# Joining the recurrence's triangular inverse to 128 rows, and applying it in one product per unit

## The reference, cut to what matters

```python
def step(state, inp):
    r_t, w_t, k_t, v_t, kk_t, b_t = inp
    sa = jnp.einsum('bhij,bhj->bhi', state, kk_t)
    state = (state * w_t[:, :, None, :]
             - sa[..., None] * b_t[:, :, None, :]
             + v_t[..., None] * k_t[:, :, None, :])
    y = jnp.einsum('bhij,bhj->bhi', state, r_t)
    return state, y
```

## Time and profile before

| | |
|---|---|
| median of 3 runs | 1575.68 us (1571.98 to 1575.98) |
| profiled execution: its time, its span | 1576.64 us, 1574.4 us |
| PE busy | 1473.1 us, 94% of the span |
| DVE, ACT, POOL busy | 739.1, 604.9, 464.0 us |
| mean granted clock of PE | 0.943 of full |
| recurrence, stages 15 to 22, batch 1 | about 148 to 177 us from the span's start |
| the same, batch 2 | about 298 to 376 us |

### The profile page before, as it was taken

One profiled execution on the slowest core, in us unless ns is written; L12 is line 12 of the kernel. 1 busy time (PEld: TensorE's weight loads), 2 busy tenths in 40 slices (PEclk: granted clock), 3 DMA queues, 4 the chain that ended last, 5 costly groups with the idle time before them and its releaser, 6 DMA issues.

```text
span 1574.4 us, 19313 instructions
## 1 busy us (share of the span) xinstructions
PE 1473.1 (94%) x7736; PEld 1154.6 (73%) x7736; DVE 739.1 (47%) x1156; ACT 604.9 (38%) x948; POOL 464.0 (29%) x162
## 2 busy tenths in 40 slices
PE   6999997899879999999998999999999988699995
PEld 5878876688668888888876887666687867577762
DVE  3356277733353532515132596334352335566663
ACT  4443245322353332323134124533333444255552
POOL 2352122000225664646423444320134520200002
PEclk9999998657899999999998999999999999799998
DMA  6232112000135445354432333200123521889964
GB/s 209 87 121 68 56 66 95 2 1 1 46 129 160 135 146 159 124 158 142 139 107 80 98 112 99 80 27 27 49 85 107 188 58 67 346 314 422 419 261 188
DMA packets 97803, 203.90 MB, mean 130 GB/s; under 512 B 6672, under 2 KB 56208, under 8 KB 91056
## 3 DMA queue, kind: packets, MB, share of 16 engines
q1 hardware_dynamic: 90656, 176.94, 32.6%
q10 hardware_dynamic: 4752, 17.30, 2.7%
q0 software_dynamic: 2304, 8.39, 1.4%
HBM read 168.54 MB, written 34.08 MB: 129 GB/s over the span
## 4 chain that ended last, share of the span: by engine, by line
PE 83%; DVE 6%; ACT 5%; issue 3%; DMA 2%; POOL 1%; SPq 0%; POOLq 0%; DVEq 0%; ACTq 0%
PE bank L517 21%; PE bank L499 12%; PE bank L501 12%; PE bank L500 12%; PE bank L2770 4%; PE bank L780 3%; PE bank L799 3%; PE bank L790 2%; PE bank L1193 2%; PE bank L782 1%; ACT whi L428 1%; PE bank L706 1%; PE bank L2716 1%; PE bank L1149 1%; PE bank L1252 1%
## 5 line engine op out<-in xcount | busy, mean ns | idle before, releaser
L436 POOL TENSOR_TENSOR wlo<-raw,whi 128x2048 fp32r<-128x2048 f32 (+2 forms) x83 | 378.7, 4562 | 698.1 <-ACT whi L428 672.0
L428 ACT ACTIVATE whi<-raw 128x2048 fp32r<-128x2048 f32 (+1 forms) x84 | 159.1, 1894 | 279.6 <-PE bank L501 272.1
L517 PE MATMUL bank<-alo,whi 128*128 128x512 f32 x368 | 149.5, 406 | 4.9 <-DVE alo L728 4.9
L1986 DVE TENSOR_TENSOR ffn_relu<-ffn_relu 128x512 f32<-128x512 f32 x32 | 97.7, 3052 | 107.0 <-ACT ffn_relu L1966 107.0
L517 PE MATMUL bank<-ahi,whi 128*128 128x512 f32 x368 | 146.5, 398 | 0.0
L499 PE MATMUL bank<-alo,whi 128*128 128x512 f32 (+1 forms) x360 | 141.1, 392 | 0.0
L501 PE MATMUL bank<-ahi,wlo 128*128 128x512 f32 (+1 forms) x360 | 140.3, 390 | 0.0
L500 PE MATMUL bank<-ahi,whi 128*128 128x512 f32 (+1 forms) x360 | 140.1, 389 | 0.0
L517 PE MATMUL bank<-ahi,wlo 128*128 128x512 f32 x368 | 91.7, 391 | 0.0
L517 PEld LDWEIGHTS bank<-alo,whi 128*128 128x128 f32 x368 | 71.3, 194 | 23.5 <-DVE alo L728 6.1
L517 PEld LDWEIGHTS bank<-ahi,whi 128*128 128x128 f32 x368 | 71.4, 194 | 15.5 <-issue 0.7
(11 more groups left out here) (483 smaller groups left out, 3005.2 us busy)
## 6 DMA issues: line engine op xcount, KB each, us to landing
raw<-in_w_in_dram SPq DMA_DIRECT2D x18, 1024.0 KB, 5.1
expert_gate_up<-in_expert_w_gate_dram SPq DMA_DIRECT2D x17, 1024.0 KB, 11.8
expert_gate_up<-in_expert_w_up_dram SPq DMA_DIRECT2D x17, 1024.0 KB, 14.2
expert_down<-in_expert_w_down_dram SPq DMA_DIRECT2D x17, 1024.0 KB, 9.2
raw<-in_w_ffn_up_dram SPq DMA_DIRECT2D x16, 1024.0 KB, 6.2
raw<-in_w_ffn_down_dram SPq DMA_DIRECT2D x16, 1024.0 KB, 5.6
raw<-in_w_in_first_dram SPq DMA_DIRECT2D x12, 1024.0 KB, 5.5
expert_rows_dram<-zero_rows SPq DMA_DIRECT2D x23, 512.0 KB, 6.9
```

The lines of the kernel that those rows point to most:

```text
L428: nc.scalar.activation(whi[:, n % SPLIT, 0:k * c], raw[:, n % RAW, 0:k * c], ACT.Copy).then_inc(hi_made, 1)
L436: nc.gpsimd.tensor_tensor(wlo[:, n % SPLIT, 0:k * c], raw[:, n % RAW, 0:k * c], whi[:, n % SPLIT, 0:k * c].bitcast(F32), ALU.subtract).the ...
L517: ins = nc.tensor.matmul(acc, of, by, start=first and i == 0, stop=last and i == products - 1)
L1986: nc.vector.tensor_tensor(relu2[:, n % 2, :], relu[:, n % 2, :], relu[:, n % 2, :], ALU.mult).then_inc(up_sq, 1)
```

## The change

The inverse of each unit is now joined to 128 rows (`inverse_t`, 128 columns for each unit, one buffer for each pair in place of the shared `inv64_t`), and then applied once:

- Stage 16: "merge" makes the 16-column product for three quarters in place of two (8 more matmuls for each pair); DVE's "inv_low" is one instruction of 96 rows in place of two of 32.
- "diagonal": eight ACT instructions of 32x256 in place of four of 32x512. Upper zeros: six POOL memsets in place of two, and POOL waits for "bv" (stage 10) first.
- Stage 18: "x" is computed already transposed, and DVE copies in place of transposing. PE also computes its other orientation for the first half ("x_rows", 8 matmuls of 32x32 for each pair), which ACT copies, after a copy of `inv`, into `minus_t`.
- Stage 19: "t64", 16 matmuls with 64-column weights and 32 moving columns (8 over 64 rows, 8 over 32 rows), copied by ACT ("minus_t64").
- Stage 20: "x64", 8 matmuls 64x64 with 64 moving columns, copied by DVE ("below64").
- Stage 21: "w", 8 matmuls of 128x128 with 128 moving columns into two banks, copied by ACT in two instructions of 128x512.
- "w0", "r", "w1" (8 matmuls each for each pair), their four ACT copies and DVE's two "rest" additions go. The numbers of stages and the fills stay; each pair plans one PSUM bank less.

The core of the diff (left out: the import, the lists of step names, and the bank plan, which follows the list above):

```diff
...
             b.spread = wk(9).rearrange("p (i a j) -> p i a j", i=SMALL, a=2)
-            b.turned = wk(4).rearrange("p (m n) -> p m n", n=BLOCK)
+            b.turned = [wk(n).rearrange("p (m n) -> p m n", n=BLOCK) for n in (4, 5)]
+            b.inverse_t = wk(4, 2).rearrange("p (u n) -> p u n", u=8)
             b.ktok, b.btok = (wk(n).rearrange("p (c n) -> p c n", c=NCH) for n in (10, 11))
...
             b.cross = b.beta[:, 256:512].rearrange("p (u n) -> p u n", u=8)
+            b.minus_t64 = b.beta[:, 0:512].rearrange("p (u n) -> p u n", u=8)
...
         turned_in = by_columns.rearrange("p i a j -> p i (a j)")
-        inv_t, inv = pairs[0].turned, pairs[1].turned
+        inv_t, inv = pairs[0].turned
         gathered = put("rw_gathered", [P, BLOCK, BLOCK])
-        inv64_t = gathered[:, :, :].rearrange("p i m -> p (i m)").rearrange("p (m n) -> p m n", m=16)
+        pairs[0].inverse_t = gathered[:, :, :].rearrange("p i m -> p (i m)").rearrange("p (u n) -> p u n", u=8)
...
             for n in range(8):
-                for qs in quarters[0::2]:
+                for qs in quarters[0:3]:
                     nc.tensor.matmul(acc[qs, n * SMALL:(n + 1) * SMALL], inv_t[qs, m0 + n, :], b.cross[qs, n, 0:SMALL], start=True, stop=True)
...
                     second = slice(s + BLOCK, s + 2 * BLOCK)
-                    ins = nc.tensor.matmul(acc[second, n * BLOCK:(n + 1) * BLOCK], inv64_t[second, m0 + n, BLOCK:2 * BLOCK], b.minus_t[second, n, :],
+                    first = slice(s, s + BLOCK)
+                    ins = nc.tensor.matmul(acc[first, n * BLOCK:(n + 1) * BLOCK], b.minus_t[second, n, :], b.inverse_t[second, n, second],
                                            start=True, stop=True)
             banks.filled(ins, u + "x")
+            acc = banks.open(pe, u + "x_rows")
+            second = slice(BLOCK, 2 * BLOCK)
+            for n in range(8):
+                ins = nc.tensor.matmul(acc[second, n * BLOCK:(n + 1) * BLOCK], b.inverse_t[second, n, second], b.minus_t[second, n, :],
+                                       start=True, stop=True)
+            banks.filled(ins, u + "x_rows")
             yield
             top, bottom = slice(0, HD), slice(HD, 2 * HD)
+            st.after("act", "x_rows")
+            acc = banks.open(pe, u + "t64")
+            for n in range(8):
+                nc.tensor.matmul(acc[bottom, n * HD:n * HD + BLOCK], b.ab[top, 0, n, bottom], b.minus_t[top, n, :], start=True, stop=True)
+                ins = nc.tensor.matmul(acc[bottom, n * HD + BLOCK:(n + 1) * HD], b.ab[second, 0, n, bottom], inv[second, m0 + n, :],
+                                       start=True, stop=True)
+            banks.filled(ins, u + "t64")
+            yield
+            st.after("act", "minus_t64")
             st.after("dve", "below")
             pe.wait_ge(*batch_at("act", p, "diagonal"))
-            pe.wait_ge(*batch_at("pool", p, "upper_zero1"))
+            pe.wait_ge(*batch_at("pool", p, "upper_zero5"))
+            acc = banks.open(pe, u + "x64")
+            for n in range(8):
+                ins = nc.tensor.matmul(acc[top, n * HD:(n + 1) * HD], b.minus_t64[bottom, n, :], b.inverse_t[bottom, n, bottom],
+                                       start=True, stop=True)
+            banks.filled(ins, u + "x64")
+            yield
+            st.after("dve", "below64")
             for i in range(2):
-                acc = banks.open(pe, f"{u}w0{i}")
+                acc = banks.open(pe, f"{u}w{i}")
                 for c in range(NCH):
-                    ins = nc.tensor.matmul(acc[top, c * P:(c + 1) * P], inv64_t[top, m0 + 4 * i + c, :], b.kb[top, i, c, :], start=True, stop=True)
-                banks.filled(ins, f"{u}w0{i}")
-            yield
-            for i in range(2):
-                st.after("act", f"w0{i}")
-                acc = banks.open(pe, f"{u}r{i}")
-                for c in range(NCH):
-                    ins = nc.tensor.matmul(acc[bottom, c * P:(c + 1) * P], b.ab[top, 0, 4 * i + c, bottom], b.neg_w[top, 4 * i + c, :],
-                                           start=True, stop=True)
-                banks.filled(ins, f"{u}r{i}")
-            yield
-            for i in range(2):
-                st.after("dve", f"rest{i}")
-                acc = banks.open(pe, f"{u}w1{i}")
-                for c in range(NCH):
-                    ins = nc.tensor.matmul(acc[bottom, c * P:(c + 1) * P], inv64_t[bottom, m0 + 4 * i + c, :], b.kb[bottom, i, c, :],
-                                           start=True, stop=True)
-                banks.filled(ins, f"{u}w1{i}")
-            yield
-            st.after("act", "w11")
+                    ins = nc.tensor.matmul(acc[:, c * P:(c + 1) * P], b.inverse_t[:, 4 * i + c, :], b.kb[:, i, c, :], start=True, stop=True)
+                banks.filled(ins, f"{u}w{i}")
+            yield
+            st.after("act", "w1")
             acc = banks.open(pe, u + "q")
...
                 act.wait_ge(*batch_at("dve", p, "inv_t"))
-                for q in range(0, P, BLOCK):
-                    qs = slice(q, q + BLOCK)
-                    at = q % (2 * BLOCK)
-                    ins = activate(inv64_t[qs, :, at:at + BLOCK], inv_t[qs, 0:16, :], ACT.Copy)
+                for i, of in enumerate(pairs):
+                    for q in range(0, P, BLOCK):
+                        qs = slice(q, q + BLOCK)
+                        ins = activate(of.inverse_t[qs, :, qs], inv_t[qs, 8 * i:8 * i + 8, :], ACT.Copy)
                 ins.then_inc(batch_done["act"], 1)
...
             yield
+            st.after("dve", "inv_low")
+            activate(b.minus_t[0:BLOCK, :, :], inv[0:BLOCK, 8 * (p % 2):8 * (p % 2) + 8, :], ACT.Copy)
+            acc = banks.take(act, u + "x_rows")
+            second = slice(BLOCK, 2 * BLOCK)
+            st.done(activate(b.minus_t[second, :, :], acc[second, 0:256].rearrange("p (u n) -> p u n", u=8), ACT.Copy), "x_rows")
+            yield
+            acc = banks.take(act, u + "t64")
+            st.done(activate(b.minus_t64[HD:2 * HD, :, :], acc[HD:2 * HD, :].rearrange("p (u n) -> p u n", u=8), ACT.Copy, scale=-1.0), "minus_t64")
+            yield
             yield
             act.wait_ge(*batch_at("dve", p, "inv"))
-            for rows in (0, 1):
-                part = slice(rows * HD, (rows + 1) * HD)
-                for i in range(2):
-                    acc = banks.take(act, f"{u}w{rows}{i}")
-                    st.done(activate(b.neg_w[part, 4 * i:4 * i + 4, :], acc[part, :].rearrange("p (u n) -> p u n", u=4),
-                                     ACT.Copy, scale=-1.0), f"w{rows}{i}")
-                yield
-                if rows == 0:
-                    yield
+            for i in range(2):
+                acc = banks.take(act, f"{u}w{i}")
+                st.done(activate(b.neg_w[:, 4 * i:4 * i + 4, :], acc[:, :].rearrange("p (u n) -> p u n", u=4), ACT.Copy, scale=-1.0), f"w{i}")
+            yield
             yield from range(4)
...
             dve.wait_ge(*batch_at("act", p, "diagonal"))
-            for q in (0, 2 * BLOCK):
-                to = inv[q:q + BLOCK, m0:m0 + 8, 0:SMALL]
-                ins = stt(out=to, in0=acc[q:q + BLOCK, 0:P].rearrange("p (u n) -> p u n", u=8), scalar=const("minus_half")[q:q + BLOCK, 0:1],
-                          in1=to, op0=ALU.mult, op1=ALU.add)
-            st.done(ins, "inv_low")
+            rows = slice(0, 3 * BLOCK)
+            to = inv[rows, m0:m0 + 8, 0:SMALL]
+            st.done(stt(out=to, in0=acc[rows, 0:P].rearrange("p (u n) -> p u n", u=8), scalar=const("minus_half")[rows, 0:1],
+                        in1=to, op0=ALU.mult, op1=ALU.add), "inv_low")
             for q in range(0, P, BLOCK):
-                at = q % (2 * BLOCK)
-                to = inv64_t[q:q + BLOCK, m0:m0 + 8, at + SMALL:at + BLOCK]
+                to = b.inverse_t[q:q + BLOCK, :, q + SMALL:q + BLOCK]
                 ins = stt(out=to, in0=acc[q:q + BLOCK, P:2 * P].rearrange("p (u n) -> p u n", u=8), scalar=const("minus_half")[q:q + BLOCK, 1:2],
...
             acc = banks.take(dve, u + "x")
-            dve.wait_ge(*batch_at("act", p, "diagonal"))
             for s in (0, 64):
                 first, second = slice(s, s + BLOCK), slice(s + BLOCK, s + 2 * BLOCK)
-                ins = nc.vector.transpose(inv64_t[first, 8 * (p % 2):8 * (p % 2) + 8, BLOCK:2 * BLOCK],
-                                          acc[second, 0:256].rearrange("p (u n) -> p u n", u=8))
+                ins = nc.vector.tensor_copy(b.inverse_t[first, :, second], acc[first, 0:256].rearrange("p (u n) -> p u n", u=8))
             st.done(ins, "below")
             yield
             yield
-            for i in range(2):
-                acc = banks.take(dve, f"{u}r{i}")
-                rest = b.kb[HD:2 * HD, i, :, :]
-                st.done(tt(rest, rest, acc[HD:2 * HD, :].rearrange("p (c n) -> p c n", c=NCH), ALU.add), f"rest{i}")
+            acc = banks.take(dve, u + "x64")
```

(27 more changed lines are left out.)

## The result

| | before | after |
|---|---|---|
| median | 1575.83 us (4 runs) | 1588.1 us (4 runs) |
| profiled execution: its time, its span | 1576.64, 1574.4 us | 1585.49, 1583.7 us |
| stages 15 to 21, batch 1 (first "cross" to first "q") | 25.8 us | 40.5 us |
| the same with "q" and its fill, batch 2 (first "cross" to first "h") | 81.2 us | 77.4 us |

The ratio is 1.0082, 95% interval [1.0067, 1.0097]: slower by some 12 us, where 1572.0 us and "same" were forecast. The profiled execution is one of the changed kernel's quicker ones, 2.6 us under its median. Between the two spans lie 9.3 us: +0.2 before the first "cross", +14.7 in batch 1, -0.5 between the batches, -3.8 in batch 2, -1.3 behind it.

What follows compares the result with a forecast made beforehand. PE's own time and its clock were taken to bound the kernel; +4.9 us in batch 1 and -8.6 in batch 2 gave -3.7, a median of 1572.0 us, range 1564.5 to 1581 (the forecast's own 1568.5 to 1575.5).

Steps and rivals of the forecast that it cites:

- t64 term: Stage 19: 64 MATMULs at 0.054 us each, 3.4 us in batch 1 (2.4 to 7); 6.9 us in batch 2.
- rival 4: t64's short products don't overlap their loads: 0.11 us for each MATMUL, about +7 us, 1583 us; chance 0.08.
- merge term: Stage 16: 32 more MATMULs in a less loaded quarter add 0.1 us (0 to 0.4).
- gaps over 0.3 us in the short stages: Sign against the forecast: PE gaps this long in any short stage, counted at nothing but those named.
- The clock in batch 1: Falls in t64, 4.5 us after x starts; w restores it after 3.5 us; 9.5 us at half, +4.4 us.
- rival 1: The clock holds in batch 1, since PE never idles there: -8.1 us, 1567.6 us; chance 0.2.
- The diagonal: Before merge: ACT's eight copies take 3.2 us, +0.7 us on PE's path, PE's gap before merge 1.35 us.
- x_rows: Stage 18: 32 MATMULs in one quarter take 1.2 us, 0.6 if they overlap as x does.
- Batch 2's clock: Returns inside w, one stage before q; w, stage 22's fill and q gain: -6.9 us (-6 to -7.5).
- x64 and w at full clock: Stages 20 and 21, batch 1 at 2.4 GHz: x64 1.7 us and w 3.45 us.

Runs made afterwards that it cites:

- t64_grouped: The changed kernel with each pair's eight 64-row matmuls of t64 first, then its eight 32-row ones; 1576.36 us, ratio 1.0016.
- joined_one_fills: joined_lean with t64 as one 64x64 product per unit and two of batch 1's fill steps moved ahead of t64 and x64; 1562.36 us, ratio 0.9928.
- merge_two: The changed kernel with merge's product and DVE's addition for two quarters, the third's correction left out; 1576.86 us, ratio 1.0014.
- joined_lean: The changed kernel with t64 grouped by rows, diagonal copies behind cross, and merge's third product replaced by a DVE transpose; 1567.49 us, ratio 0.9958.
- x_repeat: The kernel before with 32 extra MATMULs of each batch put behind x in stage 18; 1577.72 us, ratio 1.0014.
- grouped_fills: t64_grouped with two fill steps of batch 1 moved from stages 18 and 24 to 19 and 20; 1575.93 us, ratio 1.0008.
- diagonal_late: The changed kernel with ACT's diagonal copies moved behind those of cross; 1583.37 us, ratio 1.0053.

## Why the prediction was wrong

Forecast was a span shorter by 3.7 us; it is longer by 9.3, 13.0 us apart. Of these 9.8 lie in batch 1 (+14.7 for +4.9), 4.8 in batch 2 (-3.8 for -8.6), and -1.6 outside.

- **The step that failed first is the t64 term** ("half the weight columns, so 0.054 us: ... 64 x 0.054 = 3.4 us"). The pitch was 0.114 at full clock and 0.174 at half: +3.9 us in batch 1's term and +4.2 in batch 2. It was taken from q's last rows, where all matmuls have 128 rows. In t64 64 rows and 32 rows take turns, some 32 times in a batch, and the turns had no term. The pitch is the high end that I gave (0.11), and rival 4 has it with a chance of 0.08. But the rival's reason was wrong for these products. Short products do overlap their loads in groups: 0.058 us within the groups of t64_grouped, 0.061 in x64 of joined_one_fills. It is the turn from one row count to the other that costs, shown by a change of order alone. The trace of before shows that price, 0.11 us, where the fill follows merge (under t64_grouped), and I had not read it there. A rule for it stands in the Trainium skill, "TensorEngine Tiling (Array Packing)", section "Key Properties": a change of the tiling mode, as from 64 rows to 32, drains the engine. It gives no price; the trace agrees, with 0.11 us a turn. The rule on loads that I had cited knows only columns; the 0.058 within a group comes near the 53 ns that I had estimated from it, the 0.114 does not.
- **The merge term** ("+0.1 us (0 to 0.4)"): merge's own time grew by 0.2, inside the bounds, but with it came a stall of 2.31 us, a cost for which I had no term. In batch 1 five kernels beside the changed one have it, all with 224 MATMULs in a row (1.76 to 2.85 us), each with fewer than 20 of them still to come; it goes with 192 (merge_two, joined_lean), and does not come when the extra 32 stand elsewhere (x_repeat). In batch 2 the count does not decide alone, as x_repeat shows. The Trainium skill, "Runtime: NRT & Kernel Launch", section "Instruction fetch mechanics", says that each engine fetches its instructions in blocks of 16 KiB while it executes, and that this is mostly hidden; the 16 KB transfers of q8 fit such blocks, and if the fetch is what the 2.31 us wait for, as the ten stalls suggest, it was not hidden here. I had said that gaps over 0.3 us in the short stages would make the forecast wrong, "which I count at nothing".
- **The clock in batch 1.** That it falls in t64 with PE never idle was right: from 159.0 to 174.5 us it had none, and in joined_lean none from bv on. The place inside t64 has some luck in it: over the kernels where x keeps its fill ahead, the fall comes 3.0 to 6.0 us after x starts, and 4.5 was forecast. So rival 1 fell, and the rule that it leaned on, in the Trainium skill, "TensorE: Matmul & The Clock Gate", section "Why this matters for your kernels" (falls come from idle gaps), does not cover this stretch. That w brings it back was right as well, but after 5.1 us, not 3.5 (2.2 to 5.2 us in all these kernels), and half clock lasted 13.7 us, not 9.5. Of the 4.2 us between, 2.3 are the longer t64 and 1.6 w. At full clock t64 would take 7.3 us (64 x 0.114), x64 2.0 and w 3.8 (grouped_fills), together 13.1, and they took 18.8: 5.7 us lost to the clock, 4.7 were reckoned. Unforeseen was the first fall, at 157.4, which nearly doubled the fill: +2.3. It follows the two idle stretches of 1.52 and 2.31 us: with one of them gone it is half as long (merge_two, diagonal_late), with both gone it is absent (joined_lean).
- **The diagonal** was right: merge's gap 1.52 us for 1.35, ACT's eight copies 3.4 us for 3.2.
- **x_rows** cost less than its term, 0.65 us for 1.2: it overlaps with x.
- **Batch 2's clock** was right: back 75 us after its fall in place of 88.7, inside w, and the fill of stage 22 and q at full clock. Of the forecast's -8.6 us the t64 term took 4.2. -4.4 remain, measured -3.8.
- **Sum.** The terms of the error in batch 1: t64 3.9, stall 2.3, first fall 2.3, more of the second 1.0, x64 and w at full clock 0.6 (5.8 us for 5.15), the small ones, x_rows above all, -0.3; that is the 9.8. They do not act alone, since they share the clock: single repairs gained more than their own terms (t64_grouped 9.8 us in the two batches for 8.1, diagonal_late 3.1 in batch 1 for a pause of 1.5).

What stays open: whether the stall is the supply of instructions, which the traces suggest and no run tests; and why the clock stood at half for less time outside the stages in merge_two, which is where most of the gain beyond its stages lies.

## What to carry to other kernels

Price a matmul by the pitch of its neighbours as they will stand in the program: products of different row counts in turns cost here nearly twice what they cost in groups (0.114 us for 0.065), and regrouping was free. Look at the short instructions of a burst too: 32 more of them among 192 cost batch 1 some 4 us, a stall and the half clock behind it included, where behind x they cost 0.3 us and filled 0.3 us of a pause. A restructuring that is even in PE's work can still win once such losses are out: the same joined inverse, with t64 in one shape, no added product in merge and the copies moved, is 0.7% faster than the kernel before.

## What the runs showed of the hardware

- Alternating MATMULs of 64 and 32 rows: 0.114 us each at 2.4 GHz, 0.174 at 1.2; within groups 0.058 and 0.107. A turn costs 0.11 us at 2.4 GHz, 0.13 at 1.2, and a turn from 32 rows to 128 in the kernel before 0.11.
- In batch 1 a burst of 224 MATMULs of 32x32 with 16 moving columns stands idle for 1.8 to 2.9 us, 2 to 3 us after its start; one of 192 doesn't. In batch 2 three bursts of 192 do, for 0.5 us. All ten such stalls end 1.2 to 1.5 us after a 16 KB transfer of instructions.
- The granted clock went to half inside t64 after 15.5 us in which PE had no idle (159.0 to 174.5), and stood there through 64x64 matmuls without a gap. In joined_lean it fell in t64 with no idle of PE since bv. It came back 2.2 to 5.2 us after w, with 128 rows and 128 moving columns, had begun.
